# A two-layer conditioned mixer on one core: the layer loop written out, the first adaLN on TensorE, index scores placed among dense projections, and norms and selections reordered

## The reference

```python
shift, scale, gate = jnp.split(jax.nn.silu(c) @ w_ada + b_ada, 3, axis=-1)
h = rmsnorm(x, g_norm) * (1 + scale[:, None]) + shift[:, None]
z = h @ w_in
cq, ckv, kr, ga, qb, kb, vb, qi, ki, wi, gb, ma, mb = jnp.split(z, split_idx, axis=-1)
...
score = jnp.einsum('bqhd,bsd->bqhs', qi, ki)
idx_score = jnp.einsum('bqh,bqhs->bqs', wi, jax.nn.relu(score)).astype(jnp.float32)
idx_score = jnp.where(chunk_visible(qpos, kpos)[None], idx_score, -jnp.inf)
vals, idx = lax.top_k(idx_score, topk)
```

## Time and profile before

| | us |
|---|---|
| runs shown | 1265.05, 1255.71, 1260.36 |
| median | 1260.36 |
| span of the profiled execution | 1255.0 |
| TensorE busy in it | 1131.9 (90%) |
| VectorE, ScalarE, GpSimd busy | 783.6, 486.3, 388.6 |

### The profile page before, as it was taken

How to read it: one execution, slowest core, us unless ns; L and a number is a source line. 1 busy time by engine, 2 the same in 40 slices (tenths; PEclk the granted TensorE clock), 3 DMA queues, 4 the chain that set the end, 5 groups by cost and what they waited for, 6 DMA issues and landing times. The chain is left out here.

```text
span 1255.0 us, 20340 instructions
## 1 busy us (share of the span) xinstructions
PE 1131.9 (90%) x7644; PEld 982.9 (78%) x7660; DVE 783.6 (62%) x1626; ACT 486.3 (39%) x1088; POOL 388.6 (31%) x220
## 2 busy tenths in 40 slices
PE   3189999999999999989979999999999999988996
PEld 2067698677888888879967779777888888878995
DVE  7964899572447875254646489965235786535555
ACT  4344545532443333332324544633244343332322
POOL 5633265021122322233334235502112222223332
PEclk9589799999999999989999989999999999999998
DMA  9624022121114444113424303221111454311353
GB/s 376 220 87 132 14 88 68 55 68 34 34 34 152 153 155 155 60 40 115 166 99 128 91 19 100 64 63 47 34 42 53 156 173 152 118 51 51 110 179 150
DMA packets 39066, 128.17 MB, mean 102 GB/s; under 512 B 5736, under 2 KB 6344, under 8 KB 38128
## 3 DMA queue, kind: packets, MB, share of 16 engines
q1 hardware_dynamic: 36496, 122.04, 29.5%
q10 hardware_dynamic: 2464, 4.74, 1.0%
HBM read 117.41 MB, written 11.58 MB: 103 GB/s over the span
## 5 line engine op out<-in xcount | busy, mean ns | idle before, releaser
L688 PE MATMUL pj<-h_hi,w_hi 128*128 128x272 f32 x1776 | 526.4, 296 | 13.3 <-DVE h_lo L1488 6.1
L690 PE MATMUL pj<-h_lo,w_hi 128*128 128x272 f32 x1776 | 517.3, 291 | 0.0
L689 PE MATMUL pj<-h_hi,w_lo 128*128 128x272 f32 x1776 | 514.4, 290 | 0.0
L1591 POOL TENSOR_TENSOR w_lo<-ring,w_hi 128x1024 fp32r<-128x1024 f32 x112 | 275.6, 2461 | 584.7 <-ACT w_hi L1033 584.6
L688 PEld LDWEIGHTS pj<-h_hi,w_hi 128*128 128x128 f32 x1776 | 339.0, 191 | 17.4 <-POOL w_lo L1591 6.6
L689 PEld LDWEIGHTS pj<-h_hi,w_lo 128*128 128x128 f32 x1776 | 339.0, 191 | 0.2
L690 PEld LDWEIGHTS pj<-h_lo,w_hi 128*128 128x128 f32 x1776 | 337.7, 190 | 0.0
L1033 ACT ACTIVATE w_hi<-ring 128x1024 fp32r<-128x1024 f32 x112 | 119.1, 1063 | 144.1 <-PE pj L690 130.8
L1480 DVE CUSTOM_DVE_ANT_0 squares<-ring,silu_c 128x1024 f32<-128x1024 f32 x96 | 128.3, 1336 | 7.0 <-DMA ring<-in_wts 5.3
L1179 ACT ACTIVATE probs<-logit,negmax 128x128 f32<-128x128 f32 (+2 forms) x68 | 39.1, 575 | 198.9 <-DVE negmax L1422 184.9
L1413 DVE TENSOR_REDUCE negmax<-ps 128x1 f32<-128x128 f32 (+1 forms) x64 | 31.4, 490 | 107.1 <-PE ps L883 106.9
(11 more groups left out here) (239 smaller groups left out, 1541.6 us busy)
## 6 DMA issues: line engine op xcount, KB each, us to landing
ring<-in_wts SPq DMA_DIRECT2D x167, 512.0 KB, 3.6
wide<-x_between SPq DMA_DIRECT2D x4, 1088.0 KB, 5.6
x_between<-wide ACTq DMA_DIRECT2D x16, 272.0 KB, 2.5
wide<-in_wts SPq DMA_DIRECT2D x3, 1024.0 KB, 20.8
ring<-in_wts SPq DMA_DIRECT2D x6, 384.0 KB, 2.9
wide<-in_xT SPq DMA_DIRECT2D x1, 2176.0 KB, 13.2
x_between<-in_xT SPq DMA_DIRECT2D x1, 2176.0 KB, 9.8
bias_p<-in_wts SPq DMA_DIRECT2D x2, 1024.0 KB, 7.8
```

Of the source, the lines that this page charges most:

```text
L688: pe.matmul(out, hi, h_hi[:, k, half(b)], start=(k == first), stop=False)
L689: pe.matmul(out, lo, h_hi[:, k, half(b)], start=False, stop=False)
L690: return pe.matmul(out, hi, h_lo[:, k, half(b)], start=False, stop=(k == stop))
L1591: pool.tensor_tensor(w_lo[:, slot, :], w(*splits[n]), w_hi[:, slot, :].bitcast(F32), ALU.subtract).then_inc(s_wlo, 1)
```

## The change

It writes the loop over layers out and changes four orders.

1. **One block.** `make_layer(layer, before)` builds each layer's instructions, and one block runs both layers and y one after the other without a barrier; semaphores count on (`past`) instead of being cleared. stay_busy(40) stands between the layers only. Parameters of both layers are loaded once. Outputs of a layer are stored while the next stages run.
2. **The first adaLN on TensorE.** silu(c) is also formed on a transposed copy of c, padded to 32 columns (c_cols); four products of eight matmuls each (32 x 512, into four column groups of one bank) are copied by ACT, folded by TensorE (128 x 2) and turned into mod and amp for two channel tiles each by DVE. Two stand ahead of the lag loop, two inside it. DVE's and POOL's reduces, the broadcast of c by DMA and the copy of x between the layers' buffers in the prelude go. The bias tables are loaded later, in the first layer.
3. **Index scores.** `index_places()` makes ten groups: six of four score steps, four of two, each followed by one dense job of ga or ckv. DVE's sums follow the same groups, with one round of select(1) behind each group from the third on, and two from the seventh on.
4. **DVE behind them.** The rest of select(1), select(2), 6 rounds of select(3), the norms, 10 rounds of select(3), rope. All 17 rounds of select(4) stand in attention steps 2 to 18. The last layer has only the 8 adaLN tiles of its gate.

```diff
+def index_places():
+    after = [("ga", t, b) for t in range(4) for b in range(2)] + [("ckv", 0, b) for b in range(2)]
+    steps = [range(4 * g, 4 * g + 4) for g in range(6)] + [range(2 * g + 12, 2 * g + 14) for g in range(6, 10)]
+    return list(zip(steps, after))
...
+def ada_tiles(layer):
+    return range(24) if layer + 1 < DEPTH else range(16, 24)
...
+        def first_product(pe, j):
...
+            for a in range(2):
+                pe.wait_ge(s_first[2 * j + a], 16)
+                for k in range(4):
+                    last = pe.matmul(ada_bank(j)[32 * k:32 * k + 32, :], c_cols.rearrange("p (k g) -> p k g", k=KD)[:, 4 * a + k, :],
+                                     ada_half[2 * j + a][:, k, :], start=(a == 0), stop=(a == 1))
+            last.then_inc(s_adp, 1)
+            pe.wait_ge(s_adc, j + 1)
...
+            for q in range(4):
+                last = pe.matmul(fold_bank(j)[:, 2 * q:2 * q + 2], ada_sum[:, j % 2, P * q:P * q + P], fold[:, :],
+                                 start=True, stop=True)
+            last.then_inc(s_adf, 1)
...
-        with nc.Fori(0, DEPTH) as layer:
...
+        def make_layer(layer, before):
...
+                if layer == 0:
+                    first_pe(pe)
+                    first_product(pe, 0)
+                    first_product(pe, 1)
...
+                for step in range(KD + QI_LAG):
+                    if layer == 0 and step in (2, 4):
+                        first_product(pe, step // 2 + 1)
...
+                places = index_places()
+                for of, job in places:
+                    for n in of:
+                        index_scores(n)
+                    project(job)
...
-                    stay_busy(pe, 20)
...
+                if not final:
+                    stay_busy(pe, 40)
...
+                for g, (of, _) in enumerate(index_places()):
+                    for n in of:
+                        index_add(n)
+                    if g >= 2:
+                        select(1, 1 if g < 6 else 2, end=False)
...
+                select(1, TOPK_P // 8 - 12)
+                select(2, TOPK_P // 8)
+                select(3, 6, end=False)
...
+                select(3, TOPK_P // 8 - 6)
...
-                    select(4, TOPK_S // 8 - 7, end=False)
...
-                    select(4, 3, end=False)
...
-                        if 2 <= s < 6:
-                            select(4, 1, end=(s == 5))
+                    if 2 <= s < 2 + TOPK_S // 8:
+                        select(4, 1, end=(s == 1 + TOPK_S // 8))
...
-            nc.all_engine_barrier(sems_to_clear=range(min(nums), max(nums) + 1))
```

More of the change, by code:

```diff
@@ L28 @@
+from collections import namedtuple
 from contextlib import ExitStack
@@ L100, in weight_tiles @@
         need[tile] = second[before] + 1
-    for n in range(24):
+    for n in ada_tiles(layer):
         need["ada", n] = ADA_STEP + n
@@ new lines, in layer_pe @@
+                for s in range(NS + 3):
+                    if s < NS:
+                        scores(s)
+                    if 0 <= s - 2 < NS:
+                        turn(s - 2)
+                    if s - 3 >= 0:
+                        values(s - 3)
+                    for job in fill_at.get(s, ()):
+                        project(job)
+                for f in range(8):
+                    pe.wait_ge(s_wlo, split_no["wo", f] + 1)
+                    for b in range(2):
+                        for a, kind in enumerate(("ya", "yb")):
+                            out = bank((kind, f, b))
+                            if f == 0:
+                                pe.wait_ge(*((s_galo1 if b else s_galo, 4) if a == 0 else (s_gblo, 4 * b + 4)))
+                            for k in range(4 * a, 4 * a + 4):
+                                last = three(out[:, 0:HF], ("wo", f), k, b, 4 * a, 4 * a + 3)
+                            last.then_inc(s_full, 1)
@@ new lines, in layer_act @@
+                act.wait_ge(s_lst, past(s_lst) + 2)
+                act.activation(rstd[0].rearrange("p (b t) -> p b t", b=2), ps[:, :, 0:HF], ACT.Sqrt,
+                               bias=eps[:, :], scale=1.0 / KVL).then_inc(s_lrt, 1)
+                act.wait_ge(s_lst, past(s_lst) + 5)
+                for b in range(2):
+                    last = act.activation(rstd[1][:, half(b)], pt[b][:, 0:HF], ACT.Sqrt,
+                                          bias=eps[:, :], scale=1.0 / QL)
+                last.then_inc(s_lrt, 1)
@@ new lines, in output_hi @@
+                def output_hi(gt, chunk, tiles_of, b, ready):
+                    for t in tiles_of:
+                        act.activation(h_hi[:, chunk + t, half(b)], gt[:, t, half(b)], ACT.Copy).then_inc(ready, 1)
+                for s in range(NS + 2):
+                    if s < NS:
+                        exp(s)
+                    if s >= 2:
+                        turn_out(s - 2)
+                    if s == NS:
+                        act.wait_ge(s_oev, uses - 1)
+                        output_hi(gate_a, 0, range(4), 0, s_gahi)
+                    for job in fill_at.get(s - 1, ()):
+                        filler(job)
@@ L1657, in _ @@
             def _(dve):
+                for of in layers:
+                    of.dve(dve)
                 for k in range(KD):
@@ L1663, in _ @@
             def _(sp):
+                for of in layers:
+                    of.sp(sp)
                 for k in range(KD):
```

2275 lines of the change are left out of this document (1145 added, 1130 removed).

## The result

The changed kernel takes 1228.55 us (median of 4 runs, 1228.15 to 1229.59) against 1261.38 of the kernel before beside it: a ratio of 0.9754, 95% interval 0.9733 to 0.9775. The forecast was faster by 46 us, to 1214, in a range of 1190 to 1245; it became 33 faster. Its profiled span is 1226.4 us against 1255.0, so the traces have to explain 28.6.

The account below looks back on a forecast made before the run. TensorE was busy 1131.9 of 1255.0 us, so gains lie where it idles or lacks full clock. Terms 24 + 26 - 2 - 10 + 4 + 3.2 + 1 = 46 give 1209, 1214 as a median, range 1190 to 1245.

Parts of the forecast that it names:

- 2 us at qi1: End of prelude: TensorE enters qi1 with a younger clock than before, set at 2 us lost.
- Prelude: First adaLN moved to TensorE: qi1 starts at 61 against 87.3 us; gain 24 after the clock allowance.
- the lag loop, which stands as it was: Prelude, first h to qi1: 20.5 us kept, without the 20 warm-up matmuls; adaLN products counted separately.
- The column groups: First adaLN products: groups run side by side, 1.8 to 3.5 us each; rival that they do not: 1242, chance 0.12.
- Scores among jobs: Index scores interleaved with ten dense jobs: 46 us a layer against 59.65, gain 13 a layer, 26 for both.
- The rival of exclusion between VectorE and GpSimd: Merged score stage: exclusion costs more than their summed work, gain 5 instead of 26, about 1235 us; chance 0.14.
- Norms: Latent norms ahead of select(3)'s last ten rounds: just in time for TensorE, 0 to 3 us a layer lost, 1 taken.
- Rounds in the attention: Select(4) in attention steps 2 to 18: VectorE fits, 2.3 of 2.85 us a step; 0.4 a round, loss 5 a layer.
- VectorE becomes the bound: Rival: rounds in the attention make VectorE the bound, 20 us a layer, 1244 us; chance 0.08.
- Outputs stored mid-layer: Stores during a layer lie on a stream moving 30 to 170 GB/s: cost nothing, 2 if a weight tile is late.
- Seams: Between layers, before y, and the last layer's unused modulation: gains of 4, 3.2 and 1 us.
- Late instructions (slower): Rival: written-out layer bodies make dense matmuls come 14 ns later each, 75 us more, 1289 us; chance 0.03.

Follow-up runs that it names:

- Run 3: Changed kernel with VectorE forming h_lo of tile k - 2 ahead of the modulation in the first layer's h: 1226.25 us, ratio 0.9745.
- run 5: Changed kernel with stores behind the last weight load, select(4) rounds moved (three before rope, none at step 12), prelude h_lo first and products earlier: 1194.91 us, ratio 0.9485.
- run 2: Changed kernel with all eight matmuls of each first adaLN product in one column group instead of four: 1251.66 us, ratio 0.9935.
- run 6: Changed kernel with the index scores again in one row ahead of the ten dense jobs: 1258.82 us, ratio 0.9988.
- Run 7: Changed kernel with all 16 rounds of select(3) ahead of the norms of the latents, as before the change: 1263.97 us, ratio 1.0016.
- Run 1: Changed kernel with the five stores of a layer's outputs issued behind SP's last weight load of that layer: 1221.72 us, ratio 0.9708.
- run 8: Changed kernel with one warm-up matmul between the layers in place of 40: 1230.11 us, ratio 0.9756.
- run 4: Changed kernel with select(4)'s 17 rounds only in attention steps with a dense job, by intent, three at step 12: 1225.31 us, ratio 0.9744.

## Why the prediction was right, and where its terms were off

The range and the sign held: the gains came from the mechanisms named. The prelude and the rounds were mis-sized, the stores were priced at next to nothing, and the sum for the scores came out near the measurement on a working that was not right, which was luck. Apart from 2 us at qi1 the forecast has no term for a lower clock, which came with TensorE's waits (3.3 of the 8.5 us and 5.2 of the 10.4). The price of the rounds rests on a count of steps that two rows of the kernel before settle, the row maxima of steps 7 and 13:

```profile
277.92 0.67 DVE L1413 TENSOR_REDUCE negmax<-ps 128x1 f32<-128x512 f32 x1
...
314.07 0.69 DVE L1413 TENSOR_REDUCE negmax<-ps 128x1 f32<-128x512 f32 x1 [9.40 <-PE ps L883]
```


- **Prelude, 24 predicted, 18.2 measured.** The chain to the first h was right (30.5 predicted; the first scaled tile starts at 30.63), and the first two products cost it nothing: one lies beside the reciprocal, the other beside the first h. With the same prelude other runs have qi1 at 66.60 to 69.68, so against the one trace of before the gain is 18 to 21. The step that failed is "the lag loop, which stands as it was", with 2.5 us for each product. The loop did not stand as it was. h_lo of tile 2 is formed behind the modulation that needs product 2, so TensorE has nothing to do between its product's fold and that h_lo. Run 3 showed this link (2.3 to 3.6 us), run 5 with the copies and products in better places 12.9 us. The clock was granted at 0.76 in this loop and at 0.93 in run 5's, which has shorter gaps; no run tried the clock apart from the gaps. The 2 us set aside for a lower clock behind qi1 show in no run: from qi1 to the scores (69.17 to 95.00 in the changed kernel) the granted clock is 1.00. The column groups do run side by side (run 2).
- **Scores among jobs, 26 predicted, 25.8 measured (13.5 and 12.3).** I had 46 us a layer, the trace has 46.05, and run 6 undoes it and loses 28.5 us. That the number is so near is luck. I had put TensorE's own work at 42.8 us, VectorE and GpSimd at 43.4, and added 3 for unevenness. There is no unevenness, since TensorE has no gap; its own work is 46.05. The sample rows' scores are the main part that was mis-sized: the last groups of two steps and a job start their jobs 4.24 to 4.27 us apart (at 129.54, 133.78 and 138.04), where a job alone takes 3.08, so the eight steps cost near 5 us and not 2.7. The rival of exclusion between VectorE and GpSimd is there and costs TensorE nothing: the sums over 384 columns take 1.10 us each beside GpSimd where they took 0.62 in a row (run 6), VectorE is busy 39.3 of 46.05 us, and TensorE has no gap. The rule of the Trainium skill ("SBUF — State Buffer", section "SBUF: two separate sides"), a port pair that one of the two holds for a whole instruction, fits these rows; it fills VectorE's time and not TensorE's. The 2.16 us row, which I took for a sum with two inputs, is a product by a scalar (TENSOR_SCALAR); it too is slowed beside GpSimd, at 512 columns 2.06 us against 0.49 in run 6.
- **Norms, 1 a layer lost by the forecast, nothing measured.** "Just in time" was right: TensorE waits 1.3 us a layer for the norm, and the first layer's lead from the first gb job to step 2 stays at 31.7. Run 7 shows what the move carries: without it the merged scores' gain is gone.
- **Rounds in the attention, 5 a layer predicted, 8.5 measured.** The price of 0.3 to 0.4 us a round came from a wrong count of steps. The stretch from 259.70 to 277.90 holds seven steps, not six. The one from 277.90 to 315.00 runs from the row maximum of step 7 to that of step 13, so it holds six, not thirteen, of some 6 us each and not 2.85. So the two stretches give no price, the 2.3 of 2.85 us has no base, and it is luck that the forecast of 5 is not further off. (Steps 6 to 18 take 4.3 us each before and 5.1 after, where the prediction looked for 3.3.) The loss falls at few places: in the first layer 1.6 us each at steps 6, 12, 13 and 14, 0.9 at step 10 and 1.2 at step 16. A dense job in the step does not decide it alone, since steps 12 and 14 hold one, and steps 8 and 11, which hold none, lose 0.1 at most. Run 5, with three rounds ahead of rope, none at step 12 and fourteen spread from step 2 to step 32, shows that the rounds can stand where they cost nothing against the kernel before; what makes a place free was not tried step by step. That VectorE becomes the bound is refuted: it is busy 48.0 of 80.5 us in this stretch.
- **Outputs stored mid-layer, "nothing, and 2 if a weight tile is late", 10.4 measured.** This is the step that failed by most. I priced the stream by its rate and not by its order: the stores stand in SP's queue ahead of tiles that VectorE takes in order. Run 1 gives the 10 us back, half of it TensorE's idle time and half the lower clock behind that. Run 5, which has no store there either, still loses 4.5 us at the second place, so the stores are the cause that run 1 removes, and at that place not the only way to lose the time.
- **Seams, 4 + 3.2 + 1 predicted, 6.6 + 3.4 + 2.3 measured.** The last is 1.6 us at the end of the second layer's attention, where the unused modulation was, and 0.7 at the end of the first's. The 40 warm-ups ran at 0.19 us each (7.69 us in all), not 0.265, and run 8 shows that they hardly bind.
- **Late instructions (slower).** The pace is unchanged where nothing else changed: steps 20 to 38 take 58.6 us in both kernels, and the instruction queue moved 62 packets against 64 over the whole program.

## What to carry to other kernels

Price a moved DMA by what stands behind it in its queue, and by who takes that in order, not by the bandwidth that is free. When small work is spread over a chain that hands results between engines, its place decides: the rounds cost 8.5 us a layer in one set of steps and nothing in another, and three at a step without spare time cost 6.7. Count the steps of a stretch from the rows before pricing by it. Price a wait of TensorE with what its clock does behind it: here that was 40 to 60% of the loss at three places. Interleaving a stage that one engine paces with one that another paces can give nearly the sum of the idle times, but whatever came ahead of the next wait in the slower stage must move too (here the norms).

## What the runs showed of the hardware

Eight fp32 matmuls of 32 rows of output and 512 columns ran 3.7 times as fast in four column groups as in one (1.92 against 7.05 us for their sixteen records). The Trainium skill ("TensorE: Matmul & The Clock Gate", Part 3, "Measured speedup vs the span model") has 2.38 for three; no run here has three. VectorE's two-input sums slow down beside GpSimd (over 384 columns 1.10 against 0.62 us), and so does its product by a scalar (2.06 against 0.49), while MAX8 and its replacement do not (0.43 and 0.41 us in both places). A wait of 3.5 us of TensorE was followed by the lower clock: the 32 matmuls of the next product took 7.04 us in run 4 and 3.99 in run 5, where the wait was 0.78.
